# Weights of the mixing stage fetched one tile at a time

## What is computed

```
h = RMSNorm(x)
z = h @ w_in                       # 1024 x 8208
qa, ka, va, qg, kg, vg, rg, ag, ga, gb = split(z)
ua = differential_attention(qa, ka, va) @ w_pa
ub = gated_linear_attention(qg, kg, vg, ag) * silu(rg) @ w_pb
x += (sigmoid(ga) * ua + sigmoid(gb) * ub) @ w_o
x += (silu(RMSNorm(x) @ w_f1) * (RMSNorm(x) @ w_f3)) @ w_f2
x += sigmoid(RMSNorm(x) @ w_ple_gate) * (pe @ w_ple)
```

## Time and profile before

| | |
|---|---|
| three runs, us | 1449.77, 1451.29, 1451.31 (median 1451.29) |
| the profiled execution, us | 1452.98 |
| its span, us | 1451.2 |
| mean granted TensorE clock | 0.982 |
| TensorE, weight loads, VectorE, ScalarE, GpSimd busy | 95%, 91%, 61%, 43%, 21% |
| DMA packets, bytes | 194,153, 190.61 MB |

### The profile page before, as it was taken

One profiled execution on the slowest core, in us unless ns is written; L12 is line 12 of the kernel. 1 busy time (PEld: TensorE's weight loads), 2 busy tenths in 40 slices (PEclk: granted clock), 3 DMA queues, 4 the chain that ended last, 5 costly groups with the idle time before them and its releaser, 6 DMA issues.

```text
span 1451.2 us, 24068 instructions
## 1 busy us (share of the span) xinstructions
PE 1373.6 (95%) x9750; PEld 1327.2 (91%) x9750; DVE 880.2 (61%) x1423; ACT 620.2 (43%) x1043; POOL 301.0 (21%) x353
## 2 busy tenths in 40 slices
PE   6999989998999999999898999889999999999996
PEld 4899988998999999999788989889889999999995
DVE  4767747676666555555566675566665655655554
ACT  3454533546634333334344534335374343433332
POOL 1505032150023000022531231404200400001232
PEclk9999999999999999999999999999999999999998
DMA  7755598654344544544456658975524445454441
GB/s 163 130 127 128 105 106 114 147 112 133 125 144 154 160 145 145 166 142 153 110 105 116 132 129 107 117 102 120 136 96 146 146 145 157 149 165 134 149 150 43
DMA packets 194153, 190.61 MB, mean 131 GB/s; under 512 B 9046, under 2 KB 191132, under 8 KB 194044
## 3 DMA queue, kind: packets, MB, share of 16 engines
q1 hardware_dynamic: 188848, 180.58, 52.9%
q0 software_dynamic: 2688, 7.35, 1.4%
q10 hardware_dynamic: 2508, 1.16, 0.3%
HBM read 180.40 MB, written 8.65 MB: 130 GB/s over the span
## 4 chain that ended last, share of the span: by engine, by line
PE 68%; DVE 13%; DMA 8%; POOL 5%; ACT 3%; issue 2%; SPq 0%; DVEq 0%; POOLq 0%; ACTq 0%
PE big L1196 20%; PE big L1197 20%; PE big L1198 20%; DMA w_raw<-in_w_in 7%; DVE w_lo L828 4%; POOL E L520 2%; POOL E L519 2%; PE X L1470 1%; DVE ssq L976 1%; ACT w_hi L547 1%; DVE a_msk L969 1%; POOL rot L515 1%; POOL rot L522 1%; ACT p L648 1%; PE X L1324 1%
## 5 line engine op out<-in xcount | busy, mean ns | idle before, releaser
L1196 PE MATMUL big<-x_hi,w_hi 128*128 128x320 f32 x1984 | 634.6, 320 | 31.2 <-DVE z L916 12.2
L1197 PE MATMUL big<-x_lo,w_hi 128*128 128x320 f32 x1984 | 619.4, 312 | 0.0
L1198 PE MATMUL big<-x_hi,w_lo 128*128 128x320 f32 x1984 | 619.2, 312 | 0.0
L828 DVE TENSOR_TENSOR w_lo<-w_raw,w_hi 128x1024 fp32r<-128x1024 f32 (+1 forms) x328 | 416.8, 1273 | 144.7 <-ACT w_hi L547 142.5
L547 ACT CAST w_hi<-w_raw 128x1024 fp32r<-128x1024 f32 (+1 forms) x328 | 330.2, 1035 | 205.9 <-DMA w_raw<-in_w_in 110.5
L1196 PEld LDWEIGHTS big<-x_hi,w_hi 128*128 128x128 f32 x1984 | 378.9, 191 | 39.5 <-issue 16.9
L1197 PEld LDWEIGHTS big<-x_lo,w_hi 128*128 128x128 f32 x1984 | 378.7, 191 | 2.5
L1198 PEld LDWEIGHTS big<-x_hi,w_lo 128*128 128x128 f32 x1984 | 378.4, 191 | 0.0
L473 POOL TENSOR_TENSOR sqt<-xT 128x320 f32<-128x320 f32 x48 | 50.2, 1046 | 618.7 <-DVE xT L1149 422.5
L1196 PE MATMUL big<-h_hi,w_hi 128*128 128x320 f32 x352 | 108.8, 309 | 0.0
L1198 PE MATMUL big<-h_hi,w_lo 128*128 128x320 f32 x352 | 108.6, 309 | 0.0
(11 more groups left out here) (231 smaller groups left out, 1755.0 us busy)
## 6 DMA issues: line engine op xcount, KB each, us to landing
w_raw<-in_w_in SPq DMA_DIRECT2D x128, 512.0 KB, 8.4
w_raw<-in_w_f SPq DMA_DIRECT2D x120, 512.0 KB, 4.4
w_raw<-in_w_pb SPq DMA_DIRECT2D x16, 512.0 KB, 4.5
w_raw<-in_w_pa SPq DMA_DIRECT2D x16, 512.0 KB, 4.4
w_raw<-in_w_o SPq DMA_DIRECT2D x16, 512.0 KB, 4.3
w_raw<-in_w_ple_gate SPq DMA_DIRECT2D x16, 512.0 KB, 4.7
w_raw<-in_w_f SPq DMA_DIRECT2D x16, 384.0 KB, 3.7
k_raw<-in_cache_k SPq DMA_DIRECT2D x8, 256.0 KB, 9.6
```

The costliest lines, as they stand in the source:

```text
L828: tt(w_lo[:, t % 4, 0:nk, :], w_raw[:, (t // 2) % 2, 0:nk, (t % 2) * P:(t % 2 + 1) * P], w_hi[:, t % 4, 0:nk, :].bitcast(F32), ALU.subtrac ...
L1196: mm(out, wh, xh[:, k0 + k, :], start=start and k == 0, stop=False)
L1197: mm(out, wh, xl[:, k0 + k, :], start=False, stop=False)
L1198: last = mm(out, wl, xh[:, k0 + k, :], start=False, stop=stop and k == nk - 1)
```

## The change

Every transfer of the mixing stage fetches one tile: 8 chunks of 128 columns, 512 KB in runs of 512 bytes. It has its own wait, for the tile that was four before it in the same slot of `w_raw`, and its own semaphore of four, `tile_in[t % 4]`. ScalarE's cast in the mixing stage waits for the 16 counts of its own tile. The other stages keep `unit` and `raw_in`; only their counts are worked out anew. The number of transfers and their order on SyncE, with the small loads between them, are the same.

```diff
--- before.py
+++ after.py
@@ -247,6 +247,7 @@
 
 
     raw_in = [sem("raw_in0"), sem("raw_in1")]
+    tile_in = [sem(f"tile_in{i}") for i in range(4)]
     consts_in = sem("consts_in")
     tables_in = sem("tables_in")
     par_in = sem("par_in")
@@ -390,30 +391,34 @@
                 sp.dma_start(w_raw[:, c % 2, r:r + nrow // 2, :],
                              src[:, bass.ds(row0 + r, nrow // 2), bass.ds(col0, UW)]).then_inc(raw_in[c % 2], 16)
 
-        def qk_unit(tb, l, j):
-
-            sp.wait_ge(lo_ready, tb + (CREDIT_TILE - 2))
-            for half, col in enumerate((C_QG, C_KG)):
-                sp.dma_start(w_raw[:, 0, :, half * P:(half + 1) * P],
-                             w_in[:, bass.ds(l * KC, KC), bass.ds(j * P + col, P)]).then_inc(raw_in[0], 16)
+        def mix_tile(tb, t, l, col):
+
+            sp.wait_ge(lo_ready, tb + (t - 3 + CREDIT_TILE))
+            sp.dma_start(w_raw[:, t // 2 % 2, :, t % 2 * P:(t % 2 + 1) * P],
+                         w_in[:, l * KC:(l + 1) * KC, col:col + P]).then_inc(tile_in[t % 4], 16)
+
+        def mix_unit(tb, c, l, col):
+            mix_tile(tb, 2 * c, l, col)
+            mix_tile(tb, 2 * c + 1, l, col + P)
 
         for l in range(0, DEPTH):
             sp.dma_start(ga2[:, None, :], w_ga2[:, bass.ds(l, 1), :]).then_inc(ga2_in, 16)
             for j in range(0, MIX_IT):
                 tb = sp.snap(l * TILES + j * MIX_N)
-                qk_unit(tb, l, j)
-                unit(tb, 1, w_in, l * KC, KC, j * UW + C_K)
+                mix_tile(tb, 0, l, j * P + C_QG)
+                mix_tile(tb, 1, l, j * P + C_KG)
+                mix_unit(tb, 1, l, j * UW + C_K)
                 sp.wait_ge(x_trans, KC)
                 sp.wait_ge(xsum_ready, 6)
                 sp.dma_start(k_raw[:, :, :], cache_k[:, bass.ds(l * 2, 2), bass.ds(j * UW, UW)]).then_inc(k_raw_in, 16)
-                unit(tb, 2, w_in, l * KC, KC, j * UW + C_Q)
-                unit(tb, 3, w_in, l * KC, KC, j * UW + C_VG)
-                unit(tb, 4, w_in, l * KC, KC, j * UW + C_V)
+                mix_unit(tb, 2, l, j * UW + C_Q)
+                mix_unit(tb, 3, l, j * UW + C_VG)
+                mix_unit(tb, 4, l, j * UW + C_V)
                 sp.dma_start(v_past[:, :, :], cache_v[:, bass.ds(l * 2, 2), bass.ds(j * UW, UW)]).then_inc(v_past_in, 16)
                 sp.dma_start(s_past[:, None, :], state_in[:, bass.ds(l * GH + j, 1), :]).then_inc(s_past_in, 16)
-                unit(tb, 5, w_in, l * KC, KC, j * UW + C_RG)
-                unit(tb, 6, w_in, l * KC, KC, j * UW + C_GA)
-                unit(tb, 7, w_in, l * KC, KC, j * UW + C_GB)
+                mix_unit(tb, 5, l, j * UW + C_RG)
+                mix_unit(tb, 6, l, j * UW + C_GA)
+                mix_unit(tb, 7, l, j * UW + C_GB)
             for j in range(0, MRG_IT):
                 tb = sp.snap(l * TILES + j * MRG_N + MRG_0)
                 unit(tb, 0, w_pb, l * KC, KC, j * UW)
@@ -542,7 +547,11 @@
     def _(act):
         def hi(tb, tb8, t, nk):
 
-            act.wait_ge(raw_in[(t // 2) % 2], tb8 + 32 * (t // 4 + 1))
+            l, n = divmod(tb + t, TILES)
+            if n < MRG_0:
+                act.wait_ge(tile_in[t % 4], 16 * ((l * MRG_0 + n) // 4 + 1))
+            else:
+                act.wait_ge(raw_in[(t // 2) % 2], 32 * ((l * (TILES - MRG_0) + n - MRG_0) // 4 + 1))
             act.wait_ge(tile_done, tb + (t + 1))
             nc.scalar.copy(w_hi[:, t % 4, 0:nk, :], w_raw[:, (t // 2) % 2, 0:nk, (t % 2) * P:(t % 2 + 1) * P]).then_inc(hi_ready, 1)
```

## The result

The changed kernel takes 1463.27 us (median of 5 runs, 1459.05 to 1464.57) against 1451.31 (5 runs, 1449.77 to 1452.54): 12.0 us or 0.8% by the medians. The ratio on record is 1.0059, 95% interval 1.0042 to 1.0077; the five times lie in two groups, two near 1459 and three near 1464, so the loss is 0.6 to 0.8%. It is slower, as forecast, but 2.5% was forecast (1487).

What follows compares the result with a forecast made beforehand. Third mixing iterations were held bound by how fast `w_in` bytes arrive, with TensorE busy nearly throughout the second. Per layer, 2 + 6.4 + 8 + 5.3 = 21.7 less 4 in reserve, 17.7; two layers 35.4, so 1487 us, range 1442 to 1550.

Steps and rivals of the forecast that it cites:

- Both signs that the prediction named for being wrong: Mixing stage: 512-byte pairs landing under 9.9 us, seen as unchanged 79 us iterations, or a third iteration getting shorter.
- Earlier issue: Mixing stage: even tiles start one tile earlier, about 4.9 us; could give back at most 17.6 us, taken as 0.
- The seven stretches of the old query and key pairs: Existing 512-byte transfers at L397, 7.2 to 14.4 us a pair, together 72.4; used to price the new form.
- A second term put at nothing: SyncE's issue of transfers: 0.5 us in the median, up to 2.3 us with a full queue, counted as nothing.
- The price of the runs: Mixing transfers: 10.3 us for a pair in 512-byte runs against at most 8.6 in 1 KB runs.
- Tiles in reserve: Mixing stage: tiles already loaded absorb some of the added cost once in each layer, taken as 4 us.
- The upper bound of the third iteration: Third iterations: seven large pairs of 11.7 us, dearer by the ratio 10.3/8.6 = 1.20, 16 us; 8 taken.
- The 16%: Unaligned `w_in` rows: two 512-byte runs need 5.5 transactions against 4.75; 13 us a layer, 1477 us in all.
- Only the third iteration pays: Rival: 512-byte cost hidden under TensorE's 9.9 us except in third iterations; 12 us a layer, 1475 us; chance 0.15.
- The transfers stay hidden: Rival: iterations 1, 2 and 4 don't move, nor the third if held by bytes alone; 1451 us; chance 0.08.
- The earlier start pays: Rival: in third iterations even tiles are rounded half a pair earlier, 9 us back, 1442 us; chance 0.20.
- The dear pairs are the rule: Rival: mixing pairs typically cost 13.5 to 14.4 us, near 1660, or 1565 with pairs of 12; chance 0.12.

## Why the prediction was wrong in size

**Direction and place.** Slower was right, and the packets rose by 57,345 for the 57,344 forecast. ScalarE's wait for `w_in` did not rise to 200 us: 115.1 after 110.5. Both signs that the prediction named for being wrong came: the second iterations stayed at 79 us, and the third one of layer 1 got shorter, 92.29 and 90.93 after 96.81 (one profile of the kernel before).

**The step that failed** is *Earlier issue*: "I take 0, since their transfers run back to back at full DMA share", with 17.6 us as the most it could give back. It gives back 25 to 29 us. Two things were wrong in it. The bound was taken from the lengths before the change, but what is given back comes out of the new, longer iterations. It was too low even for the old ones: cut at the first matmul, the third iterations are 8.1 and 17.8 us over the second, 26 and not 17.6, and reading other columns there saved 25 (1427.6 after 1452.3). And the full DMA share, which made more transfers in flight look useless, was that of 1 KB runs. With 512-byte runs in pairs the share in a slow iteration is 0.57 and 0.71, in the changed kernel 0.59 and 0.77. What shows that there was something to gain is not the share, though, but the two runs: more transfers in flight are worth 20 us and a wait on one's own tile 16. That a transfer waits for its slowest part shows in the semaphore events of the kernel after: of the 14 single tiles issued from 174 to 262 us, the first of the 16 counts comes 13.9 us after the issue in the median, and the last 19.9. The seven stretches of the old query and key pairs had shown a share of 0.44 to 0.83; the prediction names it in favour of two rivals and does not hold it against this step.

A second term put at nothing did not stay as it was: the issue of a transfer, which took up to 2.3 us, takes up to 8.3 for a single tile in the third iteration of layer 0.

**The price of the runs** came out right only as a sum: 35.4 forecast, 36 measured by the runs alone. Its terms did not. Second iterations +6.4 forecast, 0 measured (79.05 and 78.98): a price of 10.3 for a pair doesn't matter where the queue stands empty between pairs. In the run with pairs one is issued at 107.1 us and is in at 117.5, and the next is issued at 118.4; the DMA share there is 0.51. The fourth, +5.3: 0 in layer 0, 6 in layer 1. The first, +2: 0.7 and 1.5 (91.90 and 92.14 us). The third, 8: 24.6 and 4.9 us, against an upper bound of 16. So the price belongs to the slow columns, and that the sum came out was luck: the errors cancelled. Tiles in reserve (4) were not seen as a term.

**The upper bound of the third iteration** used a ratio of 1.20. Over eight slow iterations it measured 1.18. The 16% that I had from the Trainium skill, DMA: Bandwidth & Descriptors, How a descriptor splits into AXI transactions, lies near that too; no run here changed the alignment, so the cause of the 18% is not shown to be that.

**The rivals.** *Only the third iteration pays* (1475, given 0.15) had the place right. In size it is no nearer than no change at all (1451), as the runs cost 29.5 us there and not 24, and the earlier issue, which it leaves out, gave much of that back. *The transfers stay hidden* holds in the iterations with fast columns. *The earlier start pays* named a real effect, larger than its price of 9. It does not outweigh the runs in layer 0 (24.6 us dearer by the runs, then 10 to 13 given back), but it does in the third iteration of layer 1 (4.9, then 9 to 11). *The dear pairs are the rule* is out.

**The range** of 1442 to 1550 holds the time; the likeliest value lay 24 us over it.

**Why third iterations are slow** is shown as far as the columns. Their seven pairs of 256 columns start 512 columns into a part of 1,024. Wherever an iteration stands, it gets slow when it reads them (with 1 KB runs the first, second and fourth ones take 90.7 to 97.9 us with them and 78.9 to 91.2 with their own). The query and key pair of the third iterations lies elsewhere, and its stretches of 7.2 and 8.0 us are the two shortest of the seven. That `w_in` is slow at all stands in the profile's part 6, 8.4 us against 4.4. The Trainium skill, DMA: Bandwidth & Descriptors, Latency and other measured facts, reports copies between HBM tensors that are slow at row pitches of 2 to 8 MiB, and that at 4 MiB 192 bytes of padding don't help. A row of `w_in` is 32,768 + 64 bytes, a far smaller pitch, and no run here changed it, so that this is the cause is not shown. What makes one quarter of the columns slower than the others stays open, and so does why 512-byte pairs lose 24.6 us in layer 0 and 4.9 in layer 1.

## What to carry to other kernels

Before pricing more or earlier transfers at nothing because the DMA engines are full, ask whether the change itself alters that share: here it went from 0.91 and 0.88 in the third iterations to 0.59 and 0.77, while fewer bytes per second moved. Take the answer from a run with that part alone, as the share compares badly between run lengths. Cut a slow stage at the same instruction in every iteration; one that differs from its equals although it issues the same work points to its data, and reading other columns there tests it in one run. When slow data can't be avoided, spread them: the order of heads and gates, with the new transfers, came out 15 to 18 us under the kernel before, where the new transfers alone lost 7 to 12.

## What was not expected of the hardware

With 1 KB runs, one column block of `w_in` came at 79 to 98 GB/s, for slice after slice, with a DMA share of 0.9 or more; with 512-byte runs at 46 to 82 GB/s with the engines busy for less of the time. And SyncE was held in single issues. The issue of `v_past` took 8.04 us in the third iteration of layer 0, where it took 2.3 in the kernel before. Those of the 14 single tiles issued there took 3.4 us in the median and up to 8.3. Held issues are not of the changed form alone: with 512-byte pairs they took up to 7.3 us there, and before up to 2.5. This is the source view of line 397 of the kernel after, from 174 to 262 us.

```profile
L397 SPq DMA_DIRECT2D w_raw<-in_w_in x14: 368/3438/8285, 174.8 to 259.6; - x14
...
DMA to landing us min/median/max: 10.8/19.9/28.5
```

What these held issues cost was not tried by itself.
